# Expert blocks of 64 rows taken in pairs: one gather, paired transposes and one PSUM group for two blocks

## Chip, core and metric

The kernel runs on one core of one Trainium2 chip. The metric is the device time of one execution in microseconds. The kernel before took 1452.19 us as the median of three runs (1449.91 to 1455.84).

## What is computed

Two layers of a streaming encoder over T = 544 tokens of D = 1024 channels in fp32 (512 prompt tokens and 32 sample tokens). Layer 0 mixes tokens by causal pooling, layer 1 by chunked band attention with 16 heads. Behind each mixer stands the same mixture of experts, where most of the time goes: 32 experts in 4 groups, each token goes to the best group and there to its two best experts.

```python
def run_block(args):
    tok, e = args
    xb = xpad[tok]
    hidden = jax.nn.silu(xb @ w_gate[e]) * (xb @ w_up[e])
    return hidden @ w_down[e]
# w_gate, w_up: (1024, 512) an expert, w_down: (512, 1024)
y = segment_sum(yb * row_gate[:, None], row_tok, num_segments=T + 1)[:T]
```

Every expert's three matrices are read once a layer: 3 x 2 MB x 32 experts x 2 layers = 403 MB of fp32.

## The kernel before

The kernel is written by hand: each engine has its own program, and semaphores order the programs. The order of instructions on each engine is the order in which they are written.

**Tiles.** Tokens lie in `x` in NT = 5 tiles: four of 128 rows and one of 32. Each expert owns one block of BLK = 64 row slots (544 x 2 / 32 = 34 of them are used on average); an overflow block is run only where an expert has more than 64 tokens (`n_ovf`).

**Block b on the engines.**
- GpSimd gathers the block's normalised rows from HBM (`gather`, L678, indirect DMA L692) into one of two buffers `xg[u]`, partitions 0 to 63 each.
- TensorE transposes them to PSUM bank 0 (`block_transposes`, L1780, eight 64x128 pieces), ScalarE copies them to `xT` (`xT_out`, L938).
- `gate_up` (L1786) multiplies with the gate matrix (out on partitions 64 to 127) and the up matrix (0 to 63); both write bank 1.
- ScalarE takes silu (L970), VectorE multiplies with the gate weight and the up half (`gated`, L1436), TensorE transposes the result (`hidden_transposes`, L1804, four pieces), ScalarE copies (`hidT_out`, L943).
- `down` (L1795) writes bank 3; its two column halves lie on the two partition halves. ScalarE and VectorE take it out as a high part and a rest (`y_out`, L949 and L1398).
- VectorE builds a one-hot matrix of slots against tokens (`one_hot`, L1419), and TensorE multiplies it with both parts for each of the five token tiles (`rows_to_tokens`, L1810: four matrix instructions for a tile, alternating between row halves). VectorE adds each tile's 128x1024 result to `x` (`add_rows`, L1425). The PSUM banks for this are two pairs, `Z_BANKS`.

**Order on TensorE.** `body` (L1858) of block b runs: hidden transposes of b-1; three of eight steps of gate/up of b; one-hot products of b-2 for tiles 0 and 1; the other five steps; products for tiles 2 and 3; x transposes of b+1; product for tile 4; down of b-1. The last block's down is cut in four, with the products of block 30 between; those of block 31 follow in `last_rows` (L1937), in layer 0 partly inside the first projection of the attention (`first_product`, L1993), after filler products (`keep_busy`, L1997) that use no data.

**Weights.** SyncE issues all weight loads, 2 MB each. There are three buffers for each of gate, up and down. The loads of gate and up of block b are issued when gate/up of b-3 is done (`gu_ps`, L614), the load of down of b-1 when down of b-4 is done (`y_ps`, L618). So up to six more loads stand in the DMA queues behind the one that is running.

**Names in the profile.** `ring`, `pair`, `third_pair` and `qk` are the weight buffers (block 31 uses `pair` for gate and up), `nat` holds gathered rows, silu and hidden rows, `hot` the one-hot matrices.

Of the kernel before, what the change touches and what calls it, by code (L numbers as in the profile page):

```python
# [14 lines left out]
P = 128  # L15
# [11 lines left out]
BLK = 64  # L27
# [54 lines left out]
def encoder(nc, A, O, cols):  # L82
# [32 lines left out]
    with ctx:  # L115
# [39 lines left out]
        idx_gather = sb("idx_gather", [BLK, NB], I32)  # L155
# [4 lines left out]
        gcol = [sb(f"gcol{u}", [BLK, 1], I32) for u in range(2)]  # L160
# [12 lines left out]
        xg = [nat[0:BLK, u * D:(u + 1) * D] for u in range(2)]  # L173
# [16 lines left out]
        hidden = nat[0:BLK, 4 * D + FE:4 * D + 2 * FE]  # L190
# [160 lines left out]
        gathered = [[sem(f"gathered{l}_{u}") for u in range(2)] for l in range(L)]  # L351
# [95 lines left out]
        XT_BANK, GU_BANK, HT_BANK, Y_BANK = 0, 1, 2, 3  # L447
# [4 lines left out]
        LOGIT_BANKS, INDEX_BANK, TABLE_BANK = (6, 4), 2, 3  # L452
# [69 lines left out]
        def last_bank(l, i):  # L522

            return 2 * (i % 4) if l == 1 else 2 * min(i, 2)

        def finished(i):

            return NT * (NEXP - 1) + i + 1
# [5 lines left out]
        def _(sp):  # L534
# [32 lines left out]
            for l in range(L):  # L567
# [26 lines left out]
                sp.wait_ge(gathered[l][0], 16)  # L594
# [34 lines left out]
                with sp.If(n_ovf > 0):  # L629

                    sp.wait_ge(y_ps, l * NEXP + NEXP)
# [37 lines left out]
        def _(pool):  # L669
# [8 lines left out]
            def gather(l, j, v, half, stage):  # L678

                if stage >= 2:  # L680

                    pool.wait_ge(gathered[l][v], half * 16)
                if stage == 2:

                    pool.wait_ge(table_sb, l + 1)
                if stage >= 2:
                    pool.tensor_copy(gcol[v][:, :], idx_gather[:, bass.ds(j, 1)]).then_inc(gcol_set[l], 1)

                    pool.wait_ge(xT_ps[l], j - 1)
                pool.wait_ge(gcol_set[l], j + 1)  # L690
                pool.sem_inc(wait_carrier, 1)
                pool.indirect_dma_start(  # L692
                    out=xg[v], out_offset=None, in_=xn_dram[l],
                    in_offset=bass.IndirectOffsetOnAxis(ap=gcol[v][:, :], axis=0),
                    bounds_check=XROWS - 1, oob_is_err=False).then_inc(gathered[l][v], 16)

            def experts(l):
# [4 lines left out]
                for u in range(2):  # L702
                    last = pool.memset(xg[u], 0.0)
                last.then_inc(zeroed, 1)
# [4 lines left out]
                gather(l, 0, 0, 0, 0)  # L709

                def body(b, par, half, stage):
                    if stage < NEXP - 1:

                        gather(l, b + 1, 1 - par, half + par, stage + 1)

                blocks(pool, body)
                n_ovf = pool.value_load(ovf_count[0:1, 0:1], min_val=0, max_val=OVF)
                with pool.If(n_ovf > 0):

                    for u in range(2):  # L720
                        pool.wait_ge(gathered[l][u], 16 * (NEXP // 2))
                    pool.wait_ge(xT_ps[l], NEXP)
                    with pool.Fori(0, n_ovf) as j:
                        pool.tensor_copy(gcol[0][:, :], idx_gather[:, bass.ds(j + NEXP, 1)]).then_inc(o_col[l], 1)
                        pool.wait_ge(o_col[l], j + 1)
                        pool.sem_inc(wait_carrier, 1)
                        pool.indirect_dma_start(
                            out=xg[0], out_offset=None, in_=xn_dram[l],
                            in_offset=bass.IndirectOffsetOnAxis(ap=gcol[0][:, :], axis=0),
                            bounds_check=XROWS - 1, oob_is_err=False).then_inc(o_gathered[l], 16)  # L730

                        pool.wait_ge(o_pe[l], j * 4 + 2)
                        pool.sem_inc(wait_carrier, 1)
# [87 lines left out]
        def _(act):  # L821
# [116 lines left out]
            def xT_out(l, b, u):  # L938

                act.wait_ge(xT_ps[l], b + 1)  # L940
                act.activation(xT[:, u, :], ps[:, XT_BANK, :], ACT.Copy).then_inc(xT_sb[l], 1)  # L941

            def hidT_out(l, b):  # L943

                act.wait_ge(hidT_ps[l], b + 1)
                act.activation(hidT[:, :], ps[:, HT_BANK, 0:FT * BLK], ACT.Copy).then_inc(hidT_sb[l], 1)

            def y_out(l, j, v, half, stage):  # L949

                act.wait_ge(y_ps, j + (l * NEXP + 1))
                if stage >= 2:

                    act.wait_ge(z_ps[l], j * NT - NT)
                act.activation(y_high[v], ps[:, Y_BANK, :], ACT.Copy).then_inc(y_hi[l], 1)  # L955

            def experts(l):
                xT_out(l, 0, 0)

                def body(b, par, half, stage):  # L960
# [10 lines left out]
                    if stage < NEXP - 1:  # L971
                        xT_out(l, b + 1, 1 - par)

                blocks(act, body)
                y_out(l, NEXP - 2, 0, NEXP // 2 - 1, NEXP - 2)
                hidT_out(l, NEXP - 1)
                y_out(l, NEXP - 1, 1, NEXP // 2 - 1, NEXP - 1)
                act.wait_ge(table_sb, l + 1)
                n_ovf = act.value_load(ovf_count[0:1, 0:1], min_val=0, max_val=OVF)
                with act.If(n_ovf > 0):  # L980
                    with act.Fori(0, n_ovf) as j:
# [5 lines left out]
                        act.activation(silu, ps[BLK:P, GU_BANK, :], ACT.Silu).then_inc(o_act[l], 1)  # L987
                        act.wait_ge(o_pe[l], j * 4 + 3)
                        act.activation(hidT[:, :], ps[:, HT_BANK, 0:FT * BLK], ACT.Copy).then_inc(o_act[l], 1)
                        act.wait_ge(o_pe[l], j * 4 + 4)  # L990
                        act.activation(y_high[0], ps[:, Y_BANK, :], ACT.Copy).then_inc(o_act[l], 1)
# [6 lines left out]
            split_att(0)  # L998
# [4 lines left out]
            for t in range(NT + 1):  # L1003
                if t < NT:
                    act.wait_ge(z_sb[0], finished(t))
                    root_mean_square(2, t, rows_h[0:ROWS[t], t, :])
# [1243 lines left out]
```

## Time and profile before

| | |
|---|---|
| three runs, median | 1452.19 us |
| profiled execution | 1454.51 us |
| its span, first to last instruction | 1452.7 us |
| mean granted TensorE clock | 0.988 of 2.4 GHz |
| busy: TensorE / VectorE / ScalarE / GpSimd | 97% / 50% / 21% / 11% |
| HBM traffic | 459.64 MB, 316 GB/s over the span |

The span falls in six parts: pooling layer and routing to about 80 us; experts of layer 0 to about 575; attention to about 905; routing of layer 1 to about 955; experts of layer 1 to about 1449; stores of the result.

Times in the timeline are microseconds from the first instruction. A matrix product in fp32 shows as several records, and since products overlap, their starts say more than their durations: a part's time is read from the start of the first product of its kind to the start of the next kind. A wait is shown in brackets behind the instruction that waited, with the engine that released it. A DMA is shown when it is issued; "to landing" is the time from then until its semaphore has its full count.

### The profile page before, as it was taken

Reading aid. Unit: us, or ns where it says so; the run is one execution under the profiler, and the core shown is the slowest. Engines: PE = TensorE matmul, PEld = TensorE weight load, DVE = VectorE, ACT = ScalarE, POOL = GpSimd, SP = SyncE. Lnnn points to the kernel's source line nnn. Section 1 sums busy time; section 2 is a strip of 40 time slices with the busy share of each in tenths; the row PEclk is TensorE's granted clock in tenths of the full one; section 3 lists DMA queues with packets and bytes.
Section 4 is the critical chain, followed back from the end, with each engine's and each line's share of the span. In section 5 each row is a group of like instructions: output and inputs, shape, how many; then the busy total and the mean of one; then the engine's idle time right before and its main releaser. Section 6 shows DMA issues by size and latency. Waiting matters only on the chain. (4 is left out here: it accounts for less than half of the span.)

```text
span 1452.7 us, 20574 instructions
## 1 busy us (share of the span) xinstructions
PE 1405.6 (97%) x7564; PEld 709.5 (49%) x7564; DVE 724.9 (50%) x1159; ACT 304.9 (21%) x638; POOL 159.9 (11%) x263
## 2 busy tenths in 40 slices
PE   8999999999999998999998999999999999999996
PEld 7744444444444443678776644644444444444442
DVE  3634544545445456455416643535445554454455
ACT  3211111111111113244326442211111111111110
POOL 1010000000000001023423220010000000000000
PEclk8999999999999999999999999999999999999998
DMA  9599999999999997211138321999999999999993
GB/s 368 231 349 405 407 398 404 407 409 411 402 407 408 399 417 280 73 58 69 52 98 268 92 48 61 405 347 403 399 407 410 401 407 405 408 407 391 407 417 123
DMA packets 51122, 459.64 MB, mean 316 GB/s; under 512 B 8269, under 2 KB 9549, under 8 KB 25978
## 3 DMA queue, kind: packets, MB, share of 16 engines
q1 hardware_dynamic: 38030, 425.35, 73.0%
q0 software_dynamic: 10384, 25.06, 5.6%
q10 hardware_dynamic: 2652, 8.45, 1.7%
q8 instruction: 40, 0.66, 0.2%
q14 instruction: 16, 0.13, 0.0%
HBM read 455.42 MB, written 11.26 MB: 321 GB/s over the span
## 5 line engine op out<-in xcount | busy, mean ns | idle before, releaser
L1428 DVE TENSOR_TENSOR x<-x,ps 128x1024 f32<-128x1024 f32 (+1 forms) x320 | 378.6, 1215 | 355.1 <-PE ps L1816 355.0
L1816 PE MATMUL ps<-y_parts,hot 64*128 64x512 f32 (+1 forms) x1280 | 197.2, 417 | 14.9 <-DVE y_parts L1405 6.4
L1816 PEld LDWEIGHTS ps<-y_parts,hot 64*128 64x128 f32 (+1 forms) x1280 | 98.6, 170 | 138.8 <-issue 120.3
L1791 PE MATMUL ps<-ring,xT 128*64 128x512 f32 x352 | 160.0, 598 | 2.3 <-ACT xT L941 1.6
L1792 PE MATMUL ps<-pair,xT 128*64 128x512 f32 x352 | 161.7, 603 | 0.0
L1791 PE MATMUL ps<-pair,xT 128*64 128x512 f32 x352 | 161.7, 603 | 0.0
L1792 PE MATMUL ps<-ring,xT 128*64 128x512 f32 x352 | 160.0, 598 | 0.0
L1800 PE MATMUL ps<-qk,hidT 128*64 128x512 f32 x336 | 154.4, 599 | 1.9 <-DVE y_parts L1405 1.9
L1801 PE MATMUL ps<-qk,hidT 128*64 128x512 f32 x336 | 154.5, 599 | 0.0
L692 POOL DMA_INDIRECT nat<-xn,gcol x64 | 61.9, 968 | 803.6 <-PE ps L1783 746.5
L1791 PE MATMUL ps<-third_pair,xT 128*64 128x512 f32 x320 | 145.8, 598 | 0.4 <-DMA third_pair<-in_moe_w_up 0.4
L1792 PE MATMUL ps<-third_pair,xT 128*64 128x512 f32 x320 | 145.9, 598 | 0.0
L970 ACT ACTIVATE nat<-ps 64x512 f32<-64x512 f32 x64 | 38.1, 595 | 503.6 <-PE ps L1792 503.6
L1405 DVE TENSOR_TENSOR y_parts<-ps,y_parts 128x512 fp32r<-128x512 f32 x64 | 44.3, 692 | 114.4 <-ACT y_parts L955 114.4
L955 ACT ACTIVATE y_parts<-ps 128x512 fp32r<-128x512 f32 x64 | 38.2, 597 | 253.2 <-PE ps L1801 253.2
L1791 PEld LDWEIGHTS ps<-ring,xT 128*64 128x64 f32 x352 | 44.7, 136 | 86.9 <-issue 85.6
L1791 PEld LDWEIGHTS ps<-pair,xT 128*64 128x64 f32 x352 | 45.1, 137 | 86.1 <-issue 84.6
L1800 PEld LDWEIGHTS ps<-qk,hidT 128*64 128x64 f32 x336 | 42.0, 136 | 90.4 <-issue 90.4
L1801 PE MATMUL ps<-ring,hidT 128*64 128x512 f32 x176 | 80.2, 598 | 0.0
L1800 PE MATMUL ps<-ring,hidT 128*64 128x512 f32 x176 | 80.2, 598 | 0.0
L1642 PE MATMUL ps<-w_hi,hT_hi 128*128 128x512 f32 x192 | 77.3, 403 | 2.1 <-DVE nat L1531 1.4
L1791 PEld LDWEIGHTS ps<-third_pair,xT 128*64 128x64 f32 x320 | 40.5, 136 | 77.6 <-issue 76.3
(227 smaller groups left out, 1922.4 us busy)
## 6 DMA issues: line engine op xcount, KB each, us to landing
qk<-in_moe_w_down SPq DMA_DIRECT2D x42, 2048.0 KB, 25.3
ring<-in_moe_w_down SPq DMA_DIRECT2D x22, 2048.0 KB, 26.4
pair<-in_moe_w_gate SPq DMA_DIRECT2D x22, 2048.0 KB
pair<-in_moe_w_up SPq DMA_DIRECT2D x22, 2048.0 KB, 27.4
ring<-in_moe_w_gate SPq DMA_DIRECT2D x20, 2048.0 KB, 21.1
ring<-in_moe_w_up SPq DMA_DIRECT2D x20, 2048.0 KB
third_pair<-in_moe_w_gate SPq DMA_DIRECT2D x20, 2048.0 KB, 20.5
third_pair<-in_moe_w_up SPq DMA_DIRECT2D x20, 2048.0 KB
```

The lines of the kernel that those rows point to most:

```text
L692: pool.indirect_dma_start(out=xg[v], out_offset=None, in_=xn_dram[l], in_offset=bass.IndirectOffsetOnAxis(ap=gcol[v][:, :], axis=0), bound ...
L955: act.activation(y_high[v], ps[:, Y_BANK, :], ACT.Copy).then_inc(y_hi[l], 1)
L970: act.activation(silu, ps[BLK:P, GU_BANK, :], ACT.Silu).then_inc(silu_sb[l], 1)
L1405: V.tensor_tensor(y_rest[v], ps[:, Y_BANK, :], f32(y_high[v]), ALU.subtract).then_inc(y_lo[l], 1)
L1428: return V.tensor_tensor(x[0:n, i, :], x[0:n, i, :], ps[0:n, bank:bank + 2, :].rearrange("p b c -> p (b c)"), ALU.add)
L1642: mm(out, x_hi, w_h, start=start, stop=False)
L1791: mm(ps[BLK:P, GU_BANK, :], rows, gate[:, at], start=(k == 0), stop=(k == KT - 1))
L1792: last = mm(ps[0:BLK, GU_BANK, :], rows, up[:, at], start=(k == 0), stop=(k == KT - 1))
L1800: mm(ps[0:BLK, Y_BANK, :], rows, slot[:, at:at + 512], start=(k == 0), stop=(k == FT - 1))
L1801: last = mm(ps[BLK:P, Y_BANK, :], rows, slot[:, at + 512:at + D], start=(k == 0), stop=(k == FT - 1))
L1816: last = mm(ps[0:n, bank + hf, :], hot[v][slots, tok(i)], part[slots, :], start=(part is y_high[v]), stop=(part is y_rest[v]))
```

## The change

Blocks 2m and 2m+1 form pair m.

- **Gather.** One indirect DMA of 128 rows fills a single buffer `xg` on partitions 0 to 127 for two blocks. Blocks 0 and 1 are still gathered by 64 rows. The next pair's gather is issued when the pair's transposes are done. The index table has one column for a pair.
- **x transposes.** In odd blocks, 16 transposes for the next pair alternate between row halves and between PSUM banks 0 and 3 (the down product's bank). Down of b-1 has to wait until ScalarE has copied bank 3 out.
- **Hidden rows.** The gated product is done in two instructions of half the size that put half of the columns on partitions 64 to 127; the four hidden transposes alternate between row halves and between banks 0 and 1. Gate/up moves to bank 2.
- **One-hot products.** Both blocks of a pair are summed in one PSUM group: eight matrix instructions a tile and one add to `x` instead of two. They run in odd blocks only; gate/up of even blocks isn't interrupted. Both one-hot matrices are built in even blocks.
- **End of a layer.** The test for overflow blocks comes ahead of hidden transposes and down of block 31. Down of 31 runs in one piece, then the products of block 30 for the first three tiles, then, behind y of block 31, the rest. In layer 0 all five tiles are done before the projection.
- **Start of attention.** Filler products begin after the second tile's add; the weight splits of ScalarE and VectorE are put between the row norms.

```diff
@@ gpsimd
+            def gather_pair(l, m):
+                pool.wait_ge(gathered[l], m * 16)
+                pool.tensor_copy(gcol[:, :], idx_gather[:, bass.ds(m, 1)]).then_inc(gcol_set[l], 1)
+                pool.wait_ge(xT_ps[l], m + 1)
+                pool.wait_ge(gcol_set[l], m + 2)
+                pool.sem_inc(wait_carrier, 1)
+                rows_in(l, xg, gcol[:, :]).then_inc(gathered[l], 16)
@@ scalar
+            def xT_pair(l, half):
+                act.wait_ge(xT_ps[l], half + 3)
+                act.activation(xT[:, 1, :], ps[:, Y_BANK, :], ACT.Copy).then_inc(xT_sb[l], 1)
+                act.activation(xT[:, 0, :], ps[:, XT_BANK, :], ACT.Copy).then_inc(xT_sb[l], 1)
...
                 blocks(act, body)
-                y_out(l, NEXP - 2, 0, NEXP // 2 - 1, NEXP - 2)
-                hidT_out(l, NEXP - 1)
-                y_out(l, NEXP - 1, 1, NEXP // 2 - 1, NEXP - 1)
-                act.wait_ge(table_sb, l + 1)
+                y_out(l, NEXP - 2, 0, EXPERT_PAIRS - 1, NEXP - 2)
                 n_ovf = act.value_load(ovf_count[0:1, 0:1], min_val=0, max_val=OVF)
...
+                hidT_out(l, NEXP - 1)
+                y_out(l, NEXP - 1, 1, EXPERT_PAIRS - 1, NEXP - 1)
@@ vector
+                    if par and stage >= 3:
+                        for i in range(2):
+                            z_add(l, half - 1, i)
...
+                    if not par and stage >= 2:
+                        one_hot(b - 2, 0)
+                        one_hot(b - 1, 1).then_inc(hot_set[l], 1)
...
+                    gated(b, silu, hidden).then_inc(hidden_sb[l], 1)
+                    if par and stage >= 3:
+                        for i in range(2, NT):
+                            z_add(l, half - 1, i)
@@ tensor
+            def pair_transposes():
+                src = xg.rearrange("s (c k) -> s k c", k=KT)
+                for k in range(KT):
+                    for u, bank in ((0, XT_BANK), (1, Y_BANK)):
+                        rows = slice(u * BLK, (u + 1) * BLK)
+                        last = nc.tensor.transpose(ps[:, bank, k * BLK:(k + 1) * BLK], src[rows, k, :], ident[rows, rows])
+                return last
...
+                    elif not par or stage == 1:
                         gate_up(par, gate_slots[s], up_slots[s]).then_inc(gu_ps, 1)
                     else:
                         gate_up(par, gate_slots[s], up_slots[s], range(3))
-                        z_product(b - 2, par, 0, stage - 2)
-                        z_product(b - 2, par, 1, stage - 2)
+                        z_product(half - 1, 0, stage)
+                        z_product(half - 1, 1, stage)
                         gate_up(par, gate_slots[s], up_slots[s], range(3, KT)).then_inc(gu_ps, 1)
-                        z_product(b - 2, par, 2, stage - 2)
-                        z_product(b - 2, par, 3, stage - 2)
-                    if stage < NEXP - 1:
-
-                        pe.wait_ge(gathered[l][1 - par], (half + par) * 16 + 16)
+                        z_product(half - 1, 2, stage)
+                        z_product(half - 1, 3, stage)
+                    if par and stage < NEXP - 1:
+
+                        pe.wait_ge(gathered[l], half * 16 + 32)
+                        pe.wait_ge(hidT_sb[l], b)
+                        if stage > 1:
+                            pe.wait_ge(y_lo[l], b - 1)
+                            pe.wait_ge(y_hi[l], b - 1)
                         pe.sem_inc(wait_carrier, 1)
-                        block_transposes(1 - par).then_inc(xT_ps[l], 1)
-                    if stage >= 2:
-                        z_product(b - 2, par, NT - 1, stage - 2)
+                        pair_transposes().then_inc(xT_ps[l], 1)
+                    if par and stage >= 3:
+                        z_product(half - 1, NT - 1, stage)
                     if stage:
+                        if par and stage < NEXP - 1:
+                            pe.wait_ge(xT_sb[l], b + 2)
                         down_block(b - 1, (s - 1) % BUFFERS, turn - (s == 0), stage - 1)
...
+                transpose_hidden(NEXP - 1, NEXP - 1)
+                down_block(NEXP - 1, (NEXP - 1) % BUFFERS, (NEXP - 1) // BUFFERS, NEXP - 1)
+
+                pe.wait_ge(hot_set[l], EXPERT_PAIRS)
+                pe.wait_ge(z_sb[l], finished(0) - 1)
+                for i in range(3):
+                    rows_to_tokens((0,), i, LAST_BANKS[i], True, False)
+                pe.wait_ge(y_lo[l], NEXP)
+                for i in range(3):
+                    rows_to_tokens((1,), i, LAST_BANKS[i], False, True).then_inc(z_ps[l], 1)
+                rows_to_tokens((0, 1), 3, LAST_BANKS[3]).then_inc(z_ps[l], 1)
+                pe.wait_ge(z_sb[l], finished(0))
+                rows_to_tokens((0, 1), 4, LAST_BANKS[4]).then_inc(z_ps[l], 1)
```

## Rows read from the trace of the kernel before

**Rows 1.** The page's sections 1 and 2: totals of engines; 40 slices, busy tenths.

```profile
PE 1405.6 (97%) x7564; PEld 709.5 (49%) x7564; DVE 724.9 (50%) x1159; ACT 304.9 (21%) x638; POOL 159.9 (11%) x263
...
DMA  9599999999999997211138321999999999999993
```

**Rows 2.** TensorE's waits from 100 to 540 us: total, times, longest.

```profile
PE ps L1783 <- DMA nat<-xn,gcol: 0.3, 1, 0.3
```

**Rows 3.** SyncE's timeline (start, us) and DMA issues (last column: us to landing), alternating.

```profile
101.35 0.38 SPq L561 DMA_DIRECT2D pair<-in_moe_w_up  x1
...
pair<-in_moe_w_up SPq DMA_DIRECT2D x1, 2048.0 KB, 14.6
...
510.67 0.43 SPq L561 DMA_DIRECT2D pair<-in_moe_w_up  x1
...
pair<-in_moe_w_up SPq DMA_DIRECT2D x1, 2048.0 KB, 34.7
...
1377.57 0.43 SPq L561 DMA_DIRECT2D pair<-in_moe_w_up  x1
...
pair<-in_moe_w_up SPq DMA_DIRECT2D x1, 2048.0 KB, 37.5
```

**Rows 4.** TensorE's timeline in layer 1: start, us, engine, line, operation.

```profile
1201.39 0.64 PE L1791 MATMUL ps<-third_pair,xT 128*64 128x512 f32 x1
...
1204.12 1.19 PE L1816 MATMUL ps<-y_parts,hot 64*128 64x512 f32 x8
...
1205.24 0.64 PE L1791 MATMUL ps<-third_pair,xT 128*64 128x512 f32 x1
...
1209.69 1.20 PE L1816 MATMUL ps<-y_parts,hot 64*128 64x512 f32 x8
...
1210.72 0.99 PE L1783 MATMUL ps<-cst,nat 64*128 64x64 f32 x8
...
1211.82 0.64 PE L1816 MATMUL ps<-y_parts,hot 64*32 64x512 f32 x4
...
1212.39 0.64 PE L1800 MATMUL ps<-qk,hidT 128*64 128x512 f32 x1
...
1215.98 0.69 PE L1807 MATMUL ps<-cst,nat 64*128 64x64 f32 x4
...
1216.60 0.64 PE L1791 MATMUL ps<-ring,xT 128*64 128x512 f32 x1
```

**Rows 5.** DMA totals of 1201:1205 (a gather under way), 1205.5:1211 (none), then q0 of 1100:1400.

```profile
DMA packets 156, 1.41 MB, mean 351 GB/s; under 512 B 50, under 2 KB 50, under 8 KB 77
...
DMA packets 166, 2.36 MB, mean 429 GB/s; under 512 B 22, under 2 KB 22, under 8 KB 22
...
q0 software_dynamic: 1520, 2.69, 2.9%
```

**Rows 6.** TensorE's timeline at the end of layer 0.

```profile
547.53 0.64 PE L1791 MATMUL ps<-pair,xT 128*64 128x512 f32 x1
...
563.75 0.61 PE L1800 MATMUL ps<-qk,hidT 128*64 128x512 f32 x1 [0.95 <-DVE y_parts L1405]
...
574.16 2.93 PE L1816 MATMUL ps<-y_parts,hot 64*128 64x512 f32 x12 [3.21 <-DVE y_parts L1405]
...
577.01 7.01 PE L1638 MATMUL ps<-cst 128*128 128x512 f32 x12
...
587.29 0.51 PE L1642 MATMUL ps<-w_hi,hT_hi 128*128 128x512 f32 x1 [0.65 <-DVE hT_lo L1210]
```

**Rows 7.** The same at the end of layer 1, and VectorE's last row.

```profile
1415.80 0.64 PE L1791 MATMUL ps<-pair,xT 128*64 128x512 f32 x1
...
1442.47 3.52 PE L1816 MATMUL ps<-y_parts,hot 64*128 64x512 f32 x20 [3.21 <-DVE y_parts L1405]
...
1443.25 6.23 DVE L1428 TENSOR_TENSOR x<-x,ps 128x1024 f32<-128x1024 f32 x5 [0.92 <-PE ps L1816]
```

**Rows 8.** Windows: busy us (instructions) by engine, PEclk, DMA share, GB/s.

```profile
576.00:578.00 2.00, 2.00 (x7) 0.86 (x4) 1.93 (x3) 1.58 (x5) 0.00 (x0) 0.50 0.00 0
```

More of the change, by code:

```diff
@@ L172, in encoder @@
         v_nat = pool_h
-        xg = [nat[0:BLK, u * D:(u + 1) * D] for u in range(2)]
+        xg = nat[:, 0:D]
         y_parts = nc.alloc_sbuf_tensor_at("y_parts", [P, 2, 2, 512], F32R, offset=nat_at + 4 * 2 * D)
@@ L350, in encoder @@
         z_sb = per_layer("z_sb")
-        gathered = [[sem(f"gathered{l}_{u}") for u in range(2)] for l in range(L)]
+        first_in = per_layer("first_in")
+        gathered = per_layer("gathered")
         xT_ps = per_layer("xT_ps")
@@ L1391, in route @@
                 dve.wait_ge(index_ps, l + 1)
-                V.tensor_scalar(idx_gather[:, :], ps[0:BLK, INDEX_BANK, 0:NB], PAD, None, ALU.add)
+                for u in range(2):
+                    V.tensor_scalar(idx_gather[u * BLK:(u + 1) * BLK, 0:EXPERT_PAIRS],
+                                    ps[0:BLK, INDEX_BANK, u:NEXP:2], PAD, None, ALU.add)
+                V.tensor_scalar(idx_gather[0:BLK, EXPERT_PAIRS:], ps[0:BLK, INDEX_BANK, NEXP:NB], PAD, None, ALU.add)
                 for u in range(2):
@@ L1802, in down, with hidden_transposes, rows_to_tokens @@
                 return last
-            def hidden_transposes():
-                src = hidden.rearrange("s (p k) -> s k p", k=FT)
-                for k in range(FT):
-                    last = nc.tensor.transpose(ps[:, HT_BANK, k * BLK:(k + 1) * BLK], src[:, k, :], ident[0:BLK, 0:BLK])
+            def hidden_transposes(rows_in):
+                for k in range(FT // 2):
+                    for u, bank in ((0, XT_BANK), (1, HT_BANK)):
+                        rows = slice(u * BLK, (u + 1) * BLK)
+                        last = nc.tensor.transpose(ps[:, bank, k * BLK:(k + 1) * BLK],
+                                                   rows_in[rows, k * P:(k + 1) * P], ident[rows, rows])
                 return last
-            def rows_to_tokens(v, i, bank):
+            def rows_to_tokens(blocks_in, i, bank, first=True, final=True):
                 n = ROWS[i]
-                for part in (y_high[v], y_rest[v]):
+                parts = [(v, part[v]) for v in blocks_in for part in (y_high, y_rest)]
+                for at, (v, part) in enumerate(parts):
                     for hf in range(2):
@@ L1847, in down_block, with body @@
                     pe.sem_inc(wait_carrier, 1)
-                    if stage == NEXP - 1:
-                        for k in range(FT):
-                            last = down(down_slots[s], range(k, k + 1))
-                            if k == FT - 1:
-                                last.then_inc(y_ps, 1)
-                            z_product(NEXP - 2, 0, k, NEXP - 2)
-                        z_product(NEXP - 2, 0, NT - 1, NEXP - 2)
-                    else:
-                        down(down_slots[s]).then_inc(y_ps, 1)
-                def body(b, par, half, s, turn, stage):
+                    down(down_slots[s]).then_inc(y_ps, 1)
+                def body(b, par, half, s, turn, stage):
+                    if stage and not par:
+                        pe.wait_ge(xT_sb[l], b + 2)
+                    else:
+                        pe.wait_ge(xT_sb[l], b + 1)
                     if stage:
                         transpose_hidden(b - 1, stage - 1)
-                    pe.wait_ge(xT_sb[l], b + 1)
                     pe.wait_ge(gate_in[s], landed(l, s, turn))
@@ L2201, in _ @@
             experts(1)
-            for i in range(NT):
-                last_rows(1, i)
 _INS = ["x_prompt", "x_sample", "cache_pool", "cache_k", "cache_v", "norm_mix", "norm_ffn", "pool_w", "pool_scale",
```

238 lines of the change are left out of this document (119 added, 119 removed).

## The prediction, written before the changed kernel ran

> **What bounds the kernel now.** I read the page's totals first. TensorE is busy for 97% of the span, and the DMA row of the same page reads 9 in all slices of both expert stages [rows 1]. Two resources that both look full say nothing about which one sets the pace, so I went to the two views that can tell them apart.
>
> The waits of TensorE over layer 0's expert stage hold one entry, of 0.3 us [rows 2]: before the change TensorE waits for nothing there. Then the weight loads. The load of a block's up matrix is issued when block b-3 is through its gate/up product, so issue times follow TensorE, and issue plus landing time is when the data is there. For block 4 of layer 0 that is 101.35 + 14.6 = 115.95, for block 31 it is 510.67 + 34.7 = 545.37 [rows 3]. The landings advance by 429.42 / 27 = 15.90 us a block, while the issues advance by (510.67 - 101.35) / 27 = 15.16, and the block period of TensorE is 1216.60 - 1201.39 = 15.21 us [rows 3, 4]. So the DMA is the slower of the two by 0.7 us a block. TensorE lives on a lead, which shrinks by 0.7 us each block; landing times grow from 14.6 to 34.7 us. The stage ends just as it runs out. Block 31's gate/up product begins at 547.53 in layer 0, 2.2 us after its weights; in layer 1 they land at 1377.57 + 37.5 = 1415.07 and the product starts at 1415.80, a lead of 0.7 us [rows 3, 6, 7].
>
> **The change in the steady state.** Of one block now, by the start times [rows 4]: first gate/up part 2.73, two one-hot products 1.12, second gate/up part 4.45, two more products 1.03, x transposes 1.10, last product 0.57, down 3.59, hidden transposes 0.62; together 15.21, or 30.42 a pair. The pair after the change:
> - the even block has no one-hot products and no x transposes: 15.21 - (1.12 + 1.03 + 1.10 + 0.57) = 11.39. Its gate/up product isn't broken up (about 0.1 saved), and four hidden transposes on alternate row halves take between 0.31 (full overlap) and 0.62 (none); I take 0.45. That gives 11.1.
> - the odd block has double products, 2 x (1.12 + 1.03 + 0.57) = 5.4, at the same number of matrix instructions as two blocks now. Sixteen x transposes cost between 1.10 (halves overlap fully) and 2.20 (not at all); the one-hot products, which alternate row halves too, run 8 in 1.12 us where each alone lasts longer, so I lean to 1.3. With gate/up 7.2, down 3.6 and hidden 0.45 it is 18.0.
>
> That is 29.1 a pair, bounds 28.7 to 30.2, or 1.3 us less. VectorE does half as many adds of 1.2 us, but it was nobody's bound; two half-size gated products and the two one-hot rows lie beside gate/up or down. The new wait for the copy out of the Y bank has ScalarE's 0.6 us to cover and lies beside the last product (now about 1.1). The gather has a single buffer now, but it is issued some 30 us ahead of its use. The first pair gather is the exception: it carries twice the rows behind the index table, so TensorE may wait 3 to 4 us in block 1 where it waits 0.3 now [rows 2]. The lead of TensorE pays for that.
>
> The 1.3 us a pair over 32 pairs would be 42 us if TensorE were the bound. It isn't: 29.1 is under the 31.8 that the DMA takes for a pair, and the saving turns into waits for up matrices. What is worth time is what happens before the DMA is saturated (nothing changed), the DMA's own pace, and what follows the last landing.
>
> **The DMA's own pace.** The bytes are the same. Between gathers the queues move 429 GB/s, while a gather is under way 351 [rows 5]. A block's weights, 3 x 2048 KB = 6.29 MB, need 14.7 us at 429, so of the 15.9 some 1.2 us belong to the gather. Its own packets take 2.9% of 300 us for 19.7 gathers, 0.44 us each [rows 5], its 0.136 MB would take 0.32 at 429; the other 0.76 us is weight packets that run slower beside it. The trace has no gather of 128 rows. Bounds: if all of it goes by the row, a pair stays at 31.8; if all but the bytes goes by the gather, it falls by 1.2 - 0.32 = 0.9 us, times 13.5 pairs and 2 layers, 24 us. Nor is a loss excluded. The slow stretch is as long as rows take to come in, 4 us, so I place nearly all of it with the rows and take only 0.44 - 0.32 = 0.12 us for each gather saved: 27 x 0.12 = 3.2 us.
>
> The Trainium skill speaks of this on the page "DMA: Bandwidth & Descriptors". Its section "The descriptor swizzle" states that partitions 0 to 63 are written through one half of the SBUF ports. Both 64-row gathers land in partitions 0 to 63, so by that rule they slow one half of the ports, and spreading a pair over 128 partitions gives half of the bytes' time back; no row of before shows ports.
>
> **After the last landing.** Before, block 31's gate/up starts at 547.53 and the last block's one-hot products at 574.16, 26.6 us later; in layer 1 it is 1415.80 to 1442.47, the same [rows 6, 7]. After the change, from the landing: start 0.25; gate/up and four double products 2.73 + 2.25 + 4.45 + 2.15 = 11.6; a wait of 0.85, as the fifth needs the add of the third, which stands behind silu and the gated product; fifth product 1.1; down 3.6; the hidden transposes with the two copies out of the Y bank, and the overflow test that is moved in front of them, 2.1 (1.6 now); down of block 31 in one piece 3.55 (7 us now, with block 30's products between its steps); two copies out 1.5. Sum 24.5 us. Half of the three first tiles' products is done in that last wait.
> - layer 1: 1415.07 + 24.5 = 1439.6 against 1442.47, 2.9 us. The five adds of 1.25 us after that and the stores stay.
> - layer 0: 545.37 + 24.5 = 569.9 against 574.16. Then the remaining products 4.0, the filler products (7.01 us now at half clock [rows 6, 8], about 5.2 at full clock, 12 steps of 0.43 to 0.45 as in gate/up), transposes 0.85 and two copies 2.6: the projection starts at 582.6 against 587.29, 4.7 us. Two products of the last tiles, 1.3 us, leave the first projection; against it stands that split, row norm and transposes share VectorE, so I count 5.3 in all. TensorE is dense in the projection and passes this on.
>
> **Sum.** 2.9 + 5.3 + 3.2 = 11.4 us. The profiled execution took 1454.51 us (its span 1452.7 and 1.8 around it); 1454.51 - 11.4 = 1443.1. The median of the three runs is 2.3 below it, which gives 1440.8.
>
> **Rivals.**
> - The gather's cost goes mostly by the gather or by the port: a pair takes 31.0 to 31.4. For it: most of its 1.2 us is not bytes. Against it: the length of the slow stretch. Gain 0.4 to 0.8 us a pair over 27 pairs, 11 to 22, and 8 from the tails: about 1429.
> - The clock. Waits for the DMA come once a pair in one piece, 31.8 - 29.1 = 2.7 us. After an idle time of 3.21 us at the end of layer 0 [rows 6] the granted clock was 0.50, that is 1.2 GHz [rows 8], and the 12 one-hot and 12 filler products behind it took 2.93 + 7.01 us, where 1.7 + 5.2 would be due: 3.0 us lost. Against it: the idle time is shorter here. If 2.7 us is enough, in the stage each fall only eats the spare time (29.1 + 3.0 = 32.1 against 31.8), but behind the last landing of each layer it costs 3.0 us. Then 1440.8 + 6.0 + 2 = 1449. The Trainium skill warns of it too ("TensorE: Matmul & The Clock Gate", section "Why this matters for your kernels": idle gaps between bursts bring half rate back).
> - Slower: the pair gather costs the weight loads more than two single ones. Twice the rows in one burst on the same 16 engines; the cost of a pair's gathers is 2 x 1.2 = 2.4 us now, and as the DMA sets the pace, each tenth more is 2.7 us over 27 pairs. From 2.7 us a pair on it outweighs the 8 us of the tails. If the slowed part of 0.76 us grows with the square of the rows, it is 2 x 0.32 + 4 x 0.76 = 3.7: 1.3 x 27 = 35 us lost, 8 gained, about 1479. For it: the slowed weight packets; against it: no idle time of the engines is seen in the slow stretches.
> - The matrix time is saved and pays in full, TensorE being the bound: 42 us and 8 from the tails give about 1402. The landing times speak against it; chance 3%.
>
> **How the numbers follow.** The forecast (pace of the DMA nearly unchanged, clock up) has 0.45, the cheaper gather 0.30, the clock 0.13, slower 0.09, full pay 0.03. A difference of 0.5%, 7 us, is about what a measurement of this kernel can tell from no change, so 1445 is one border and 1459 the other. The forecast's own range is 1433 to 1448, four fifths of its chance below 1445: faster 0.36 + 0.30 + 0.03 = 0.69. Same is 0.09, 0.11 of the clock case and 0.01 of the slower one: 0.21. Slower is 0.02 + 0.08 = 0.10. For 8 in 10 the range goes down to 1424, through most of the cheaper gather, and up to 1456, past the clock case; full pay, most of the slower case and the ends of the others are left out.
>
> **What would show it.** The landings of up matrices should still advance by 15.8 to 15.9 us a block; TensorE's waits should list the up matrices with some 1.5 to 3 us a pair in the second half of each stage; matrix work of a pair should come to 29 us; the first last-block products should start 24.5 us behind the last up landing; the granted clock should stay at 1.00 in both stages. A pace under 15.7 is the cheaper gather, above 16.1 the dearer one. An idle DMA in the stages would make the whole prediction wrong.

## Result: 4% faster where 0.8% was forecast

| | before | after |
|---|---|---|
| median of four runs each, same chip | 1451.38 us | 1395.71 us (1390.41 to 1397.27) |
| ratio, 95% interval | | 0.9605 [0.9572, 0.9638] |
| the same in a second session | 1450.8 us | 1392.15 us, ratio 0.9601 [0.9577, 0.9626] |
| profiled execution, span | 1454.51, 1452.7 | 1390.41, 1388.4 |

The forecast was 1440.8 us with a range from 1424 to 1456. The direction held, but the gain was 55.7 us in place of 11.4, outside the range.

The profile after, the page's totals, granted clock, DMA share and GB/s by slice:

```profile
PE 1318.9 (95%) x7564; PEld 663.7 (48%) x7564; DVE 585.1 (42%) x1067; ACT 299.0 (22%) x638; POOL 125.1 (9%) x201
...
PEclk9999999999999999999999999999999999999999
DMA  9789999999999997212038321899999999999993
GB/s 356 289 344 428 426 428 426 426 429 428 427 427 427 428 426 266 76 61 91 35 106 286 89 45 67 365 367 415 428 427 426 428 428 427 426 428 427 430 425 156
```

Busy shares look much as before [rows 1]: TensorE 95% in place of 97%, the DMA a row of 9s. Only the GB/s row tells the difference. The full slices of both stages have 425 to 430, but for the first of layer 1 with 415. Before, the mean was 406 between 200 and 480 us, as each gather cut a hole in it [rows 5]:

```profile
DMA packets 9108, 113.63 MB, mean 406 GB/s; under 512 B 1723, under 2 KB 1723, under 8 KB 2323
```

SyncE's timeline and DMA issues (last column: us to landing), alternating, for the gate matrices of blocks 4 and 31 of layer 0:

```profile
97.18 0.35 SPq L560 DMA_DIRECT2D pair<-in_moe_w_gate  x1
...
pair<-in_moe_w_gate SPq DMA_DIRECT2D x1, 2048.0 KB, 9.5
...
482.86 0.34 SPq L560 DMA_DIRECT2D pair<-in_moe_w_gate  x1
...
pair<-in_moe_w_gate SPq DMA_DIRECT2D x1, 2048.0 KB, 29.8
```

They land at 106.68 and 512.66: 405.98 / 27 = 15.04 us a block, where it was 15.90 [rows 3]. In layer 1 it is 15.13. A pair's weights take 30.07 us instead of 31.81.

One pair on TensorE (same columns as [rows 4]):

```profile
314.21 0.64 PE L1833 MATMUL ps<-third_pair,xT 128*64 128x512 f32 x1
...
316.94 2.10 PE L1862 MATMUL ps<-y_parts,hot 64*128 64x512 f32 x16
318.97 0.64 PE L1833 MATMUL ps<-third_pair,xT 128*64 128x512 f32 x1
...
323.41 2.10 PE L1862 MATMUL ps<-y_parts,hot 64*128 64x512 f32 x16
325.35 0.99 PE L1825 MATMUL ps<-cst,nat 64*128 64x64 f32 x16
327.09 1.10 PE L1862 MATMUL ps<-y_parts,hot 64*32 64x512 f32 x8 [0.74 <-DVE x L1451]
328.12 0.64 PE L1842 MATMUL ps<-qk,hidT 128*64 128x512 f32 x1
...
331.71 0.34 PE L1851 MATMUL ps<-cst,nat 64*128 64x64 f32 x4
331.97 0.64 PE L1833 MATMUL ps<-ring,xT 128*64 128x512 f32 x1
...
342.43 0.34 PE L1851 MATMUL ps<-cst,nat 64*128 64x64 f32 x4
342.69 0.64 PE L1833 MATMUL ps<-pair,xT 128*64 128x512 f32 x1
```

The odd block takes 331.97 - 314.21 = 17.76 us, the even one 10.72, a pair 28.48, with a wait of 0.74 in it. The waits of TensorE from 100 to 540 us (total, times, longest):

```profile
PE ps L1862 <- DVE x L1451: 11.4, 15, 1.4
PE ps L1833 <- issue: 3.7, 3, 1.7
PE ps L1842 <- DVE y_parts L1428: 1.3, 1, 1.3
PE ps L1842 <- ACT xT L943: 0.8, 1, 0.8
```

The first is the fifth tile's product, which waits for the add of the third, once in each pair. The second is a gate/up product, late in the stage only, for which the profile names no releaser. It is its weights: in run 10 such a product starts at 488.89, and the up matrix that it reads landed at 488.77. Before, there was no wait but one of 0.3 us [rows 2].

The end of layer 0 on TensorE, then the end of layer 1 with VectorE's adds:

```profile
517.63 0.61 PE L1833 MATMUL ps<-pair,xT 128*64 128x512 f32 x1 [0.78 <-issue]
...
536.58 0.61 PE L1842 MATMUL ps<-qk,hidT 128*64 128x512 f32 x1 [1.30 <-DVE y_parts L1428]
...
540.16 5.09 PE L1862 MATMUL ps<-y_parts,hot 64*128 64x512 f32 x40
...
545.18 5.42 PE L1669 MATMUL ps<-cst 128*128 128x512 f32 x12
...
553.85 0.50 PE L1673 MATMUL ps<-w_hi,hT_hi 128*128 128x512 f32 x1 [0.66 <-DVE hT_lo L1230]
```

```profile
1354.72 0.61 PE L1833 MATMUL ps<-pair,xT 128*64 128x512 f32 x1 [0.73 <-issue]
...
1377.30 5.08 PE L1862 MATMUL ps<-y_parts,hot 64*128 64x512 f32 x40
...
1379.64 6.23 DVE L1451 TENSOR_TENSOR x<-x,ps 128x1024 f32<-128x1024 f32 x5 [0.82 <-PE ps L1862]
```

With these starts and those of [rows 3, 6, 7] the 64.3 us between the two spans can be placed:

| stretch | before | after | less |
|---|---|---|---|
| to the issue of block 4's up matrix, layer 0 | 101.35 | 97.63 | 3.7 |
| to block 31's gate/up product | 446.18 | 420.00 | 26.2 |
| to the first projection | 39.76 | 36.22 | 3.5 |
| to block 4's up matrix, layer 1 (967.63; 930.90) | 380.34 | 377.05 | 3.3 |
| to block 31's gate/up product | 448.17 | 423.82 | 24.4 |
| to the end of the span | 36.9 | 33.7 | 3.2 |

The two expert stages hold 50.6 us of it, the two ends 6.7. The other 7 us lie in stretches that the change hardly touches. The first of them ends anywhere from 94.6 to 101.7 us in the profiled executions of all the runs below, and the profiled execution after is the fastest of its four.

### The profile page after: what moved, and what is told of

Its sections match the earlier page's. It is cut to its first block, busy times and chain, and to the rows that moved or that the text cites. A ratio compares the mean times of both kernels' runs of the same rounds, so it can differ in the third digit from the quotient of the medians.

```text
span 1388.4 us, 19965 instructions
## 1 busy us (share of the span) xinstructions
PE 1318.9 (95%) x7564; PEld 663.7 (48%) x7564; DVE 585.1 (42%) x1067; ACT 299.0 (22%) x638; POOL 125.1 (9%) x201
## 3 DMA queue, kind: packets, MB, share of 16 engines
HBM read 455.42 MB, written 11.26 MB: 336 GB/s over the span
## 4 chain that ended last, share of the span: by engine, by line
PE 83%; DVE 7%; issue 3%; DMA 3%; ACT 2%; DVEq 0%; SPq 0%; POOL 0%; POOLq 0%; ACTq 0%
PE ps L1833 31%; PE ps L1842 9%; PE ps L1862 8%; PE ps L1843 8%; PE ps L2233 4%; PE ps L1673 3%; DVE x L1451 3%; PE ps L1675 3%; PE ps L1674 3%; PE ps L1669 2%; DMA nat<-xn,gcol 1%; DVE nat L1465 1%; PE ps L1757 1%; PE ps L1745 1%; DMA ring<-in_rel_bias_reversed 1%
## 5 line engine op out<-in xcount | busy, mean ns | idle before, releaser
L1451 DVE TENSOR_TENSOR x<-x,ps 128x1024 f32<-128x1024 f32 (+1 forms) x160 | 189.6, 1216 | 95.6 <-PE ps L1862 94.2
L1465 DVE SCALAR_TENSOR_TENSOR nat<-nat,slot_gate,ps 64x256 f32<-64x256 f32 x128 | 85.5, 668 | 294.8 <-ACT nat L977 277.8
L1862 PE MATMUL ps<-y_parts,hot 64*128 64x512 f32 (+1 forms) x1280 | 170.6, 401 | 22.8 <-DVE x L1451 22.8
L1833 PE MATMUL ps<-ring,xT 128*64 128x512 f32 x352 | 157.8, 596 | 4.5 <-issue 2.9
L1833 PE MATMUL ps<-pair,xT 128*64 128x512 f32 x352 | 159.5, 602 | 1.8 <-issue 1.8
L1834 PE MATMUL ps<-pair,xT 128*64 128x512 f32 x352 | 159.6, 602 | 0.0
L1834 PE MATMUL ps<-ring,xT 128*64 128x512 f32 x352 | 157.9, 597 | 0.0
L1842 PE MATMUL ps<-qk,hidT 128*64 128x512 f32 x336 | 152.1, 595 | 2.6 <-DVE y_parts L1428 2.6
L1862 PEld LDWEIGHTS ps<-y_parts,hot 64*128 64x128 f32 (+1 forms) x1280 | 105.7, 168 | 100.3 <-issue 76.9
L1843 PE MATMUL ps<-qk,hidT 128*64 128x512 f32 x336 | 152.2, 595 | 0.0
L1833 PE MATMUL ps<-third_pair,xT 128*64 128x512 f32 x320 | 143.7, 597 | 3.5 <-issue 3.5
L1834 PE MATMUL ps<-third_pair,xT 128*64 128x512 f32 x320 | 143.8, 597 | 0.0
L1428 DVE TENSOR_TENSOR y_parts<-ps,y_parts 128x512 fp32r<-128x512 f32 x64 | 44.3, 692 | 179.2 <-ACT y_parts L962 179.2
L1675 PE MATMUL ps<-w_lo,hT_hi 128*128 128x512 f32 x192 | 74.9, 390 | 0.0
```

The costliest lines, as they stand in the source:

```text
L1428: V.tensor_tensor(y_rest[v], ps[:, Y_BANK, :], f32(y_high[v]), ALU.subtract).then_inc(y_lo[l], 1)
L1451: return V.tensor_tensor(x[0:n, i, :], x[0:n, i, :], ps[0:n, bank:bank + 2, :].rearrange("p b c -> p (b c)"), ALU.add)
L1465: last = V.scalar_tensor_tensor(out=out[u * BLK:(u + 1) * BLK, :].rearrange("s (k p) -> s k p", k=n), in0=act_rows[:, u * n:(u + 1) * n, : ...
L1675: return mm(out, x_hi, w_l, start=False, stop=stop)
L1833: mm(ps[BLK:P, GU_BANK, :], rows, gate[:, at], start=(k == 0), stop=(k == KT - 1))
L1834: last = mm(ps[0:BLK, GU_BANK, :], rows, up[:, at], start=(k == 0), stop=(k == KT - 1))
```

## Experiments

All ratios are to the kernel before on the same chip in the same session. "Pace" is the advance of the up matrix's landing from block 4 to block 31, divided by 27, as in [rows 3]; the first number is layer 0, the second layer 1. The kernel before has 15.90 and 15.91, the changed one 15.04 and 15.13 (by its gate matrices). The edits are shown by their main lines; index columns, waits and operand rows that change with them are left out.

**1. The kernel before, odd blocks gathered into partitions 64 to 127.**

```diff
-        xg = [nat[0:BLK, u * D:(u + 1) * D] for u in range(2)]
+        xg = [nat[u * BLK:(u + 1) * BLK, u * D:(u + 1) * D] for u in range(2)]
```

> The kernel before with one edit: blocks of odd number are gathered into partitions 64 to 127 instead of 0 to 63; still one gather of 64 rows a block. Halves theory (the weight loads are slowed because every 64-row gather writes the same half of the partitions): the landings of the weights advance by 15.4 us a block or less, where they advance by 15.9 in the kernel before. Theory of the number (each gather costs its fixed part) and theory of the rows: 15.9 as before. The time stays near 1450 in all three, since TensorE at 15.2 us a block sets the pace of that kernel; at most 1 to 2 us are won at the end of layer 1.

Measured: 1447.64 us, ratio 0.9992 [0.9974, 1.0010], pace 15.91 and 15.95, mean 405 GB/s from 200 to 480 us. Nothing changes. Neither half is dearer than the other, and using both in turn doesn't help.

**2. The changed kernel, the pair's gather issued as two of 64 rows**, to partitions 0 to 63 and 64 to 127.

```diff
-                rows_in(l, xg, gcol[:, :]).then_inc(gathered[l], 16)
+                rows_in(l, xg[0:BLK, :], gcol[0][:, :]).then_inc(gathered[l], 16)
+                rows_in(l, xg[BLK:P, :], gcol[1][:, :]).then_inc(gathered2[l], 16)
```

> The changed kernel with the pair gather issued as two gathers of 64 rows, one into partitions 0 to 63 and one into 64 to 127, one behind the other. Theory of the number: the landings go back from 15.05 towards 15.9 us a block, and the time to 1395.7 + 27 x 0.85 x 2 = about 1440. Halves theory: both halves are written within the same few us, the landings stay at 15.1 and the time at 1396. Shape theory (a gather of 64 rows is split over the DMA engines in another way than one of 128): 15.9 and 1440 as well; it is told from the number by the run with 128-row gathers for each block.

Measured: 1440.98 us, ratio 0.9951 [0.9930, 0.9972], pace 15.94 and 15.92. The slow stretch is back, some 8 us long. TensorE's waits from 100 to 550 us, the DMA totals of 7 us, from 4 us after the issue of the first of two gathers (308.25), and a window (busy us by engine, granted clock, DMA share, GB/s) behind a wait of 3.00 us:

```profile
PE ps L1839 <- issue: 18.0, 8, 3.6
...
DMA packets 289, 2.39 MB, mean 342 GB/s; under 512 B 95, under 2 KB 95, under 8 KB 159
...
328.00:330.00 2.00, 2.00 (x6) 0.61 (x4) 0.00 (x0) 0.00 (x0) 0.00 (x0) 0.50 1.00 426
```

L1839 is the gate product here. In its time and its bound this is the kernel of my forecast: all matrix work saved, the DMA's pace not. It is worth 7.7 us. The rest of the gain hangs on this one instruction. One thing differs from the forecast: after most waits of 2.8 to 3.7 us the granted clock was 0.50, that is 1.2 GHz. It cost little, as my clock rival had said for the stage. Block 31's gate/up product starts 0.8 and 0.95 us behind the landing of its weights, where 0.25 is due, so at most 0.7 us a layer is lost by it there.

**3. The kernel before, each gather with 128 index rows**, of which 64 to 127 are out of bounds and carry nothing.

```diff
-                    out=xg[v], out_offset=None, in_=xn_dram[l],
+                    out=xg_all[v], out_offset=None, in_=xn_dram[l],
```

> The kernel before, with each block's gather made 128 rows long; rows 64 to 127 are out of bounds and write nothing, so bytes and number of gathers are the same. Shape theory: the slow stretch beside a gather vanishes or shrinks, and the landings advance by 15.1 to 15.4 us a block. Number, rows and halves theories: 15.9 us as before. The time stays near 1450 in all of them, as TensorE sets the pace.

Measured: 1450.95 us, ratio 1.0014 [0.9996, 1.0033], pace 15.55 and 15.66, mean 420 GB/s in the middle of both stages. The rows with data go to the same partitions 0 to 63, as often, and the deep dip is gone: in the four microseconds from 4 us after an issue the DMA moves 406 to 436 GB/s, where it moved 315 to 384. So neither the number of gathers nor the half in which the data lands is enough to make the dip. But not all of the loss is gone. Bytes alone would give 15.04 (run 5), so by the pace 0.5 to 0.6 of 0.87 us a block stays, by the mean rate (420 against 406 before and 427 after) a third. The time stays, as TensorE never waited for the DMA in this kernel.

**4. The kernel before without the gathers of blocks 2 to 31** (their rows are left out; the experts compute with what lies in the buffers).

```diff
+                if stage >= 2:
+                    return
```

> The kernel before without the gathers of blocks 2 to 31 (their rows are those left in the buffer, so the experts' results aren't those of the reference). The price of gathers on the DMA: the landings would advance by 14.7 us if the DMA is free of them, and since this is under TensorE's 15.2, they follow TensorE. If TensorE alone sets the pace of the kernel before, the time stays within 3 us of 1451. If the DMA already costs it time, it falls by 10 us or more.

Measured: 1447.50 us, ratio 0.9986 [0.9963, 1.0008]; landings follow the issues at 15.17 and 15.19, TensorE's own period. The whole cost of the gathers, taken from the kernel before, is worth some 2 us by this run, and 5 at most by its interval. Its TensorE has no time to give.

**5. The changed kernel without the pair gathers.**

```diff
-                rows_in(l, xg, gcol[:, :]).then_inc(gathered[l], 16)
```

> The changed kernel without the pair gathers of blocks 2 to 31 (their rows are those left in the buffer, so the experts' results aren't those of the reference). If the 128-row gather costs no more than its bytes (0.136 MB at 427 GB/s, 0.32 us a block), the landings advance by 14.73 us instead of 15.04 and the time falls by 27 x 0.31 x 2 = 17 us. If the pair gather still has a hidden price, it falls by more, down to TensorE's own pace.

Measured: 1375.87 us, ratio 0.9507 [0.9482, 0.9532], pace 14.72 and 14.71: the weights alone. With the 128-row gather it is 15.04 in layer 0, 0.32 us a block more, which is what the 0.136 MB of a block's rows take at 429 GB/s; in layer 1 it is 0.42 more. The pair gather costs its bytes and little or nothing else.

**6 and 7. The kernel before with a plain transfer of 64 x 4 KB in place of each gather**, once to partitions 0 to 63, once the same bytes as 128 pieces of 2 KB to 128 partitions.

```diff
+                if stage >= 2:
+                    pool.dma_start(xg[v], xn_dram[l][0:BLK, :]).then_inc(gathered[l][v], 16)
+                    return
```

```diff
+                    pool.dma_start(nat[:, v * D:v * D + D // 2],
+                                   xn_dram[l][0:BLK, :].rearrange("s (h n) -> (s h) n", h=2)).then_inc(gathered[l][v], 16)
```

> The kernel before with every gather of blocks 2 to 31 replaced by a plain transfer of 64 rows of 4 KB to partitions 0 to 63, issued by GpSimd at the same point (fixed rows, so the experts' results aren't those of the reference). 0.262 MB a block at 428 GB/s are 0.61 us. Shape theory (64 partitions against the 128 of the weight loads are what slows the weights): the landings advance by 14.7 + 0.6 + 0.8 or more, 16.1 to 16.9. Gather theory (only the indirect transfer does it): 15.3.

> As the run before it, with the same 0.262 MB as 128 rows of 2 KB to partitions 0 to 127 (again the experts' results aren't those of the reference). Shape theory: no slow stretch, the landings advance by 15.3. Gather theory: 15.3 as well. If short rows or more packets were the cost, it would be dearer than 64 rows of 4 KB.

Measured: 1488.94 us for the first, ratio 1.0283 [1.0256, 1.0310], pace 16.66 and 16.54; 1444.98 for the second, ratio 0.9978 [0.9966, 0.9991], pace 15.36 and 15.41. By bytes alone (6.29 + 0.262 MB at 429 GB/s) 15.3 is due. So the loss needs neither indirection nor an index table, and a transfer to 128 partitions is nearly free of it. DMA totals from 200 to 480 us, first the one, then the other:

```profile
DMA packets 8622, 110.20 MB, mean 394 GB/s; under 512 B 1080, under 2 KB 1080, under 8 KB 2168
```

```profile
DMA packets 9332, 119.41 MB, mean 426 GB/s; under 512 B 1168, under 2 KB 1168, under 8 KB 2336
```

**8. The changed kernel, VectorE's add of the third tile moved ahead of the gated product**, which removes the wait of the fifth product.

```diff
+                    if par and stage >= 3:
+                        z_add(l, half - 1, 2)
...
-                        for i in range(2, NT):
+                        for i in range(3, NT):
```

> The changed kernel with one edit on VectorE: in odd blocks the add of the third tile comes ahead of the gated product, so that TensorE needn't wait 0.76 us for it before the fifth tile's products. If the landings of the weights set the end of each stage, the time stays within 4 us of the changed kernel. If TensorE sets it, 30 x 0.76 = 22 us are won.

Measured: 1390.84 us, ratio 0.9615 [0.9590, 0.9641], the same as the changed kernel. TensorE's waits from 100 to 540 us:

```profile
PE ps L1835 <- issue: 12.8, 7, 2.5
...
PE ps L1864 <- DVE x L1451: 0.6, 1, 0.6
```

The 11.4 us of waiting for the add have become 12.8 us of waiting for weights (3.7 before the edit), and the pace is still 15.13 and 15.02. After the change the DMA sets the end of both stages.

**9. As 6, the same 64 rows of 4 KB, to partitions 0, 2, ... 126.**

```diff
-                    pool.dma_start(xg[v], xn_dram[l][0:BLK, :]).then_inc(gathered[l][v], 16)
+                    pool.dma_start(nat[0:P:2, v * D:(v + 1) * D], xn_dram[l][0:BLK, :]).then_inc(gathered[l][v], 16)
```

> The kernel before, with every gather of blocks 2 to 31 replaced by a plain transfer of 64 rows of 4 KB to every second partition, 0 to 126, so the same 0.262 MB as in the two runs with 64x4 KB and 128x2 KB (the experts' results aren't those of the reference). Theory of the half (the 64 partitions 0 to 63 are what the slow stretch comes from): it is gone here, landings advance by 15.3 to 15.4 us. Theory of the split (64 rows are dealt to the 16 DMA engines in another order than the 128 partitions of a weight load, so engines write to partitions that others serve, wherever the 64 rows lie): 16 us or more, as with 64x4 KB.

Measured: 1447.08 us, ratio 0.9972 [0.9952, 0.9993], pace 15.33 and 15.34. Same rows, same size, same queue, and 1.2 to 1.3 us a block less than in 6. The theory that named 16 us or more wherever the 64 rows lie fell. DMA totals from 200 to 480 us, against 394 GB/s in 6:

```profile
DMA packets 9337, 119.69 MB, mean 427 GB/s; under 512 B 1168, under 2 KB 1168, under 8 KB 2320
```

**10. The changed kernel once more**, beside 9.

> The changed kernel as it is, once more, beside the kernel before, to compare with the run with the early add (ratio 0.9615) and to narrow the interval: ratio 0.960, time 1391.

Measured: 1392.15 us, ratio 0.9601 [0.9577, 0.9626].

**11. As 2, the two 64-row gathers to even and to odd partitions** (rows stand in the wrong slots).

```diff
-                rows_in(l, xg[0:BLK, :], gcol[0][:, :]).then_inc(gathered[l], 16)
-                rows_in(l, xg[BLK:P, :], gcol[1][:, :]).then_inc(gathered2[l], 16)
+                rows_in(l, nat[0:P:2, 0:D], gcol[0][:, :]).then_inc(gathered[l], 16)
+                rows_in(l, nat[1:P:2, 0:D], gcol[1][:, :]).then_inc(gathered2[l], 16)
```

> The changed kernel with two gathers of 64 rows for a pair, as in the run with two gathers (ratio to before 0.9951, up matrices landing every 15.93 us a block, weight transfers down to some 340 GB/s for about 9 us in each pair); the one difference is where their rows go: even partitions for one gather, odd partitions for the other, in place of partitions 0 to 63 and 64 to 127. Rows therefore stand in other slots than the index table means. Theory A (the loss comes from 64 rows written to one half of the partitions, and is gone when they are spread over both): landings advance by 15.0 to 15.2 us a block, DMA mean 424 to 429 GB/s in 200:480, ratio 0.960 to 0.964, some 1394 us. Theory B (the loss goes by the number of gathers, or by gathers of fewer than 128 rows as such): landings advance by 15.9, ratio 0.995, some 1441 us, as with the two gathers before. Between the two, 1405 to 1430 us, both would have a part.

Measured: 1395.33 us, ratio 0.9622 [0.9600, 0.9645]. The up matrices of blocks 6 and 30 of layer 0 land at 145.46 and 507.27, 15.08 us a block. DMA totals of the same 7 us after the issue of the first of two gathers (303.72):

```profile
DMA packets 351, 2.98 MB, mean 426 GB/s; under 512 B 121, under 2 KB 121, under 8 KB 185
```

342 GB/s against 426, and 1441 us against 1395, by nothing but the partitions to which two gathers write. Theory B of this run, that the loss goes by the number of gathers or by transfers under 128 rows as such, falls.

## Why the prediction was off

**What bounds the kernel: right, and the base of all the rest.** TensorE 15.21 us a block, the DMA 15.90, the lead used up at the end. Run 4 takes away the DMA's cost alone and gains some 2 us, run 2 takes away TensorE's alone and gains 7.7 us. Together they give 55.7. Before, the stage was held from both sides: TensorE had no spare time, the DMA no spare pace, and each hid the other's saving.

**The steady state on TensorE: right in kind, too dear.** Foretold 29.1 us a pair of work, bounds 28.7 to 30.2; measured 28.48 with a wait of 0.74 in it, so 27.74 of work, below the lower bound. Terms: doubled products 5.4 foretold, 2.03 + 1.94 + 1.03 = 5.0 measured; sixteen x transposes 1.3 foretold, 1.0 measured (325.35 to 327.09 without the wait of 0.74), fewer than the eight before (1.10, [rows 4]): the halves overlap fully; hidden transposes 0.45 foretold for each block, 0.26 measured. What I left out of the pair is the fifth product's wait for the add of the third; I had priced it at the end of the stage only (0.85), and it comes in every pair with 0.7 to 1.4 us. By run 8 it costs nothing, since the weights are the later ones.

**The DMA's pace: this step failed.** I read from [rows 5] that a gather costs 1.2 us: 0.32 of bytes, 0.12 of own packets, 0.76 of weight packets slowed beside it. "I place nearly all of it with the rows", was the step, and the argument was that the slow stretch is as long as rows take to come in. That argument shows when the cost falls, not what it hangs on. The two bounds, by the row and by the gather, left out the place to which the rows go, and the larger of them was 0.9 us a pair. Measured: 31.81 - 30.07 = 1.74 us a pair, which is 2 x (1.2 - 0.32), all that isn't bytes of both gathers, and twice my larger bound. Over 13.5 pairs and 2 layers 1.74 is 47 us where I had 3.2. These 43.8 us are nearly the whole miss of 44.3.

**The ends: right in sum.** From block 31's gate/up product to the x40 group of one-hot products 22.5 and 22.6 us; the forecast puts that point at 22.75 (24.5 less the start of 0.25 and the copies of 1.5). Some of that is two errors that cancel: the fifth product waited 1.4 us for 0.85 foretold, the turn to block 31's down product took 1.6 for 2.1. In layer 1 the end came 3.2 us earlier than before, counted from that product, where 2.9 was foretold from the landing; in layer 0 the projection came 3.5 earlier, plus some 2 us of slack between landing and product that are gone (2.2 us in [rows 3, 6]), against 4.7 foretold. The twelve filler products take 5.42 us, 5.2 foretold, 7.01 before.

**The rivals.** The cheaper gather (1429, chance 0.30) was the true one by its direction, and its port half by its kind, with less than half of the price (0.4 to 0.8 us a pair for 1.74). The clock rival didn't come to pass in the stages: waits of up to 1.8 us for weights and 1.4 for adds leave the granted clock at 1.00 from 100 to 580 and from 940 to 1380 us. In run 2, with the slower DMA that I had forecast, the waits are as long as 3.7 us and the clock fell, and it cost next to nothing. The wait for the first pair gather in block 1, foretold with 3 to 4 us, was 1.5 in layer 0 and 2.6 in layer 1, and up to 3.4 in run 8. Behind the 2.6 us and one more wait of 0.8 the granted clock did fall, which the slices of 35 us on the page don't show:

```profile
936.00:938.00 2.00, 2.00 (x8) 0.75 (x6) 0.00 (x0) 0.00 (x0) 0.00 (x0) 0.50 0.97 414
```

The dearer gather fell: run 5 shows little beside bytes. Full pay (1402) gave the nearest number by the wrong mechanism: TensorE isn't the bound, run 8 says so; its saving could be cashed because the DMA gained 0.87 us a block in the same edit.

**What the loss hangs on.** A transfer of 64 rows beside the weight loads is slow when all its rows lie in one half of the partitions, whichever half (before, 1, 2, 6). It isn't when it is spread over both (7, 9, 11, the change). When it is 128 rows long with data in the lower half alone (3), the deep dip is gone, but a third to two thirds of the loss stays. So 64 rows all in one half are needed for the whole of it. That much is shown. The profile has no row by DMA engine, so what happens inside is inferred.
Run 3 has a second reading. The page's total of HBM reads is 472.20 MB there and 455.42 before. The 16.8 MB between are 64 gathers x 64 rows x 4 KB, so that total counts rows out of bounds in full, although they write nothing. If they are really read, run 3's rest may be theirs in part, and not only that of the half to which the data goes. No run separates the two.

The Trainium skill has the pieces of this on the page "DMA: Bandwidth & Descriptors". "The descriptor swizzle" states that in a transfer to 128 partitions engines 0 to 7 write partitions 0 to 63 and engines 8 to 15 the others; the section "Why a DMA increments its semaphore by 16 and not by 1" states that a transfer is split over the largest number of engines up to 16 that divides the slowest dimension of both its sides; by that, 64 rows would go over all 16 too. Which of the rows then goes to which engine isn't shown by a row here. I cited the first in the prediction and drew the wrong price from it: half of the bytes' time, where the runs show 0.87 us a block, more than the 0.32 us of all of a block's bytes.

**Open.** Why 64 rows in one half slow all weight traffic, from 426 GB/s in run 11 to 342 in run 2, and whether it is a port, an engine that writes into the other half, or the order in which writes are accepted there. How run 3's rest is shared between the half and the rows out of bounds is open too.

## What to carry to other kernels

When both TensorE and the DMA look full, compare the advance of landing times with the advance of issue times before costing an edit: savings on the two sides are worth little alone and can be worth their sum and more together. Try small transfers that run beside large 128-partition loads with their rows spread over both halves of the partitions: one transfer of 128 rows did it here, and so did 64 rows to every second partition. When a cost seen in a trace is to be split between causes, list also the shape and place of the transfer, not only its count and bytes, and let the bound reach to the whole cost.

## What the runs showed of the hardware

- A plain 64 x 4 KB transfer to partitions 0 to 63 in each block cost 1.2 to 1.3 us more than the same to partitions 0, 2, ... 126 (16.66 and 16.54 against 15.33 and 15.34 us a block), a gather of 34 rows on average 0.86 us more (15.94 against 15.08).
- Index rows that are out of bounds add nothing to the bytes of the DMA queue but leave packets: run 3 has 2611 packets in the GpSimd queue from 200 to 480 us where the kernel before has 1476, at 2.43 and 2.46 MB. The page's total of HBM reads counts them in full (472.20 against 455.42 MB).
- The granted clock didn't follow the length of a wait alone. In run 2 it was 0.50 after waits of 2.83 and 3.00 us and stayed at 1.00 after waits of 3.09 and 3.36; in run 8 it fell to 0.50 after one of 2.43 and stayed at 1.00 after one of 3.02.
- Sixteen fp32 transposes of 64x128 that alternate between row halves take 1.0 us, no longer than eight on one half (1.10).
